# Third places for two page quarters, one wider score product, and a finished result moved by ScalarE

## The chip, the cores and the metric

The kernel runs on one core of one Trainium2 chip. Five engines work side by side: PE (TensorE, matrix products and transposes, with its weight loads shown apart as PEld), DVE (VectorE), ACT (ScalarE), POOL (GpSimd) and SP (SyncE, which here only issues transfers). The metric is the device time in microseconds, the median of several runs.

## What is computed

One inference step of a two-layer decoder: a short-convolution layer, then a layer of native sparse attention, for a prompt of 512 tokens and for 8 samples of 8 new tokens, each sample with 2048 past tokens in a paged cache. All in float32. The part that matters here is the sparse attention of the samples, `nsa_core` of the reference, cut down:

```python
s_c = einsum('bqgrd,bngd->bgrqn', q, kc_blk) * scale            # scores on compressed blocks
p_c = masked_softmax(s_c, blk_end <= q_pos); o_c = p_c @ vc_blk
imp_s = block sums of p_c over the heads of a group
_, idx = top_k(imp_s + forced, 16)                              # 16 blocks of 64 past tokens
s_s = einsum('bqgrd,bgqnkd->bgrqnk', q, kv_g[..., 0, :]) * scale  # selected blocks
o_s = masked_softmax(s_s) @ kv_g[..., 1, :]
s_w = einsum('bqgrd,bkgd->bgrqk', q, kvw[:, :, 0]) * scale      # window of 512 tokens
o_w = masked_softmax(s_w) @ kvw[:, :, 1]
out = gate0 * o_c + gate1 * o_s + gate2 * o_w
```

For a sample the kernel scores all 2048 past tokens and adds a mask for the blocks that were not selected, so it reads all 16 pages of a sample (128 tokens each, 256 KB with keys and values), and its window (512 tokens, 1024 KB).

## The kernel before

The program is one straight stream for each engine, with semaphores set by hand. The stages are: norms and memory keys, the convolution layer, its output product, the projections of the second layer, attention of the prompt (about 700 to 803 us of the profile), attention of the samples (803 to 964 us), the last output product and the final norm.

**The sample stage.** `sample_phase` orders it: front(0), and then for each sample t: middle(t), front(t+1), back(t). `NB` is 8, samples are 0 to 7.

- *front(t)*: PE turns (transposes) the keys of sample t in ten turn tiles, j = 0 to 9, of four transposes each. `TURNED` says of what: tiles 0, 1 are quarter 0, tiles 2, 3 quarter 1, tiles 4, 5 quarter 2, tiles 6, 7 the window, tiles 8, 9 quarter 3. A quarter is four of the 16 pages. ACT and DVE copy the turned keys from PSUM back over the pages (lines 1224 and 2436). Between them PE scores the compressed blocks, and DVE makes the selection mask (lines 2460 to 2469).
- *middle(t)*: PE's scores. First the window part, one 512-column product a head group for the window and two 64-column ones for the new tokens (`new(0)` for the selected branch, `new(1)` for the window branch); then `out_turn`, a transpose of the finished result of sample t-1 into PSUM bank 1; then quarters 2 and 3, then quarters 0 and 1 (32 instructions of 512 columns). The last pair writes banks 0 and 1, so it waits until the result of t-1 was moved out of bank 1.
- *back(t)*: PE turns the 23 tiles of probabilities and multiplies them with the values in six groups of up to four tiles; each group adds one to `sa_used`. Group 1 is compressed blocks and part of the window, groups 2 to 5 are quarters 0 to 3, group 6 the rest. A page's place is free when its group is done.

DVE's stream for one sample: masks and maxima of sample t (`masks`, lines 2479 to 2498, run inside front(t+1)), the copies and the selection mask of front(t+1), then back(t). Its back ended with four small copies (line 2531) that move the turned result from bank 1 into `HT`, the input of the output product.

**The places.** `skv(t, c)` is the memory for quarter c of sample t. Quarter 0 had three places (used by t mod 3), quarters 1, 2 and 3 two (t mod 2); the window has three. The residual stream X (2560 KB) was written to DRAM earlier and came back at 718 us, before the prompt's attention.

**The queues.** SP loads pages 0 and 1 of each quarter and the windows, POOL pages 2 and 3. Both go through their lists in order. `quad_load` (line 583) waits until sample t - 2 (or t - 3) has used the quarter: `sa_used` past that sample's group c + 2. SP's list for t = 1 to 7 was: quarters 1, 2, 3 of t, quarter 0 of t+1, window of t+1. So what SP and POOL issue once a back has come to its last groups is a train: on each queue two pages of quarters 1, 2, 3 and then two of quarter 0, on SP a window behind them. The output weights follow at the end, `load_w(B_OUT1)` and `load_w(B_OUT1 + 1)`, each when its memory is free.

Of the kernel before, what the change touches and what calls it, by code (L numbers as in the profile page):

```python
# [29 lines left out]
SEQ = 512  # L30
NB, NT = 8, 8
# [222 lines left out]
def build(nc, I, O):  # L254
    ctx = ExitStack()
    with ctx:
# [110 lines left out]
        FIRST = [four_pages(a) for a in (at(8192, 2048), at(4096, 2048), shared)]  # L367
        LATER = [[four_pages(at(o, 2048)) for o in quads] for quads in ((10240, 0, 2048), (12288, 14336, 16384))]

        def skv(t, c):  # L370

            return LATER[t % 2][c - 1] if c else FIRST[t % 3]

# [98 lines left out]
        sa_lo = [[sem(f"sa_pages01_{c}_{n}") for n in range(2 if c else 3)] for c in range(4)]  # L472
        sa_hi = [[sem(f"sa_pages23_{c}_{n}") for n in range(2 if c else 3)] for c in range(4)]
# [109 lines left out]
        def quad_load(eng, t, c, pages, loaded):  # L583

            places = 2 if c else 3
            if t >= places:
                eng.wait_ge(sa_used, START.sa_used + 6 * (t - places) + c + 2)
            for s in pages:
                page = eng.value_load(ptab[0:1, NPG * t + 4 * c + s:NPG * t + 4 * c + s + 1], min_val=0, max_val=POOL - 1)  # L589
                eng.dma_start(skv(t, c)[:, s, :], I["csel"][bass.ds(page, 1), :, :].rearrange("a p c -> (a p) c")  # L590
                              ).then_inc(loaded[c][t % places], 16)
# [13 lines left out]
        def _(sp):  # L605
# [138 lines left out]
            sp.dma_start(Xf, x_dram).then_inc(x_back, 16)  # L744
# [38 lines left out]
        def _(pool):  # L783
# [74 lines left out]
            quad_load(pool, 0, 1, range(2, 4), sa_hi)  # L858
            pool.wait_ge(pa_t, BANKS_OF_P * (UNITS - 2))
# [3 lines left out]
            pool.wait_ge(pa_mix, 6)  # L863
            quad_load(pool, 1, 0, range(2, 4), sa_hi)
            for t in range(1, NB):
                for c in range(1, 4):
                    quad_load(pool, t, c, range(2, 4), sa_hi)
                if t + 1 < NB:
                    if t == 1:
# [1112 lines left out]
        def _(dve):  # L1982
# [523 lines left out]
            def back(t, fronts):  # L2506
# [22 lines left out]
                for g in range(KVH):  # L2529
# [3 lines left out]
                    if g < 3:  # L2533
                        lk.did(ins)
# [140 lines left out]
```

## Time and profile before

| | us |
|---|---|
| median of 3 runs | 1040.93 (1040.17 to 1042.69) |
| the profiled execution | 1036.34 |
| its span, first to last instruction | 1034.7 |
| PE busy in the span | 965.7 |
| DVE, ACT, POOL busy | 599.1, 298.2, 70.6 |
| mean granted TensorE clock | 0.982 |
| data moved by DMA | 153.03 MB |

The profile is of one execution. Times in its rows are microseconds from the span's start; each row of a timeline merges instructions of one line that follow each other on an engine, with their number behind an x, and names in brackets the idle time before them and what ended it. L1275 is the line of every product, L1278 of every transpose, L590 of every page load, L737 of the windows. Ends of PE instructions are modelled, so that PE can be shown as busy while it is not at its peak.

### The profile page before, as it was taken

Reading aid. Unit: us, or ns where it says so; the run is one execution under the profiler, and the core shown is the slowest. Engines: PE = TensorE matmul, PEld = TensorE weight load, DVE = VectorE, ACT = ScalarE, POOL = GpSimd, SP = SyncE. Lnnn points to the kernel's source line nnn. Section 1 sums busy time; section 2 is a strip of 40 time slices with the busy share of each in tenths; the row PEclk is TensorE's granted clock in tenths of the full one; section 3 lists DMA queues with packets and bytes.
Section 4 is the critical chain, followed back from the end, with each engine's and each line's share of the span. In section 5 each row is a group of like instructions: output and inputs, shape, how many; then the busy total and the mean of one; then the engine's idle time right before and its main releaser. Section 6 shows DMA issues by size and latency. Waiting matters only on the chain.

```text
span 1034.7 us, 17598 instructions
## 1 busy us (share of the span) xinstructions
PE 965.7 (93%) x6530; PEld 600.6 (58%) x6530; DVE 599.1 (58%) x1356; ACT 298.2 (29%) x734; POOL 70.6 (7%) x133
## 2 busy tenths in 40 slices
PE   5999999999977999999999999989899899998997
PEld 3576676667754445566755555665555666655443
DVE  3204997797543645999914222448876667766113
ACT  4310010100143023112124221347776434435012
POOL 0000000000000000000012010310000222120000
PEclk9999999999988999999999999999999999999999
DMA  8543644554361443386522351453002878774202
GB/s 350 184 101 123 174 122 143 172 161 100 107 206 42 104 141 123 92 212 193 181 82 101 104 185 53 162 218 109 40 1 97 312 239 301 278 247 164 103 2 90
DMA packets 48879, 153.03 MB, mean 148 GB/s; under 512 B 9497, under 2 KB 23194, under 8 KB 41882
## 3 DMA queue, kind: packets, MB, share of 16 engines
q1 hardware_dynamic: 43674, 135.13, 40.8%
q0 software_dynamic: 5120, 16.78, 4.7%
q8 instruction: 52, 0.85, 0.3%
q14 instruction: 33, 0.27, 0.1%
HBM read 142.26 MB, written 17.89 MB: 155 GB/s over the span
## 4 chain that ended last, share of the span: by engine, by line
PE 78%; DVE 8%; DMA 6%; issue 4%; ACT 1%; POOLq 1%; SPq 1%; POOL 0%; DVEq 0%; ACTq 0%
PE PS L1275 70%; PE PS L1278 8%; DMA arena<-in_csel 4%; DVE arena L2190 1%; DVE arena L2396 1%; DMA arena<-in_wall 1%; POOLq L589 1%; DMA arena<-in_cmem 1%; DVE arena L2001 1%; POOL arena L590 0%; DVE arena L2033 0%; DVE arena L2034 0%; ACT arena L1188 0%; DVE arena L2401 0%; SPq L589 0%
## 5 line engine op out<-in xcount | busy, mean ns | idle before, releaser
L1275 PE MATMUL PS<-arena 128*32 128x64 f32 (+16 forms) x5436 | 833.3, 376 | 21.7 <-issue 7.4
L1275 PEld LDWEIGHTS PS<-arena 128*128 128x128 f32 (+6 forms) x5436 | 478.2, 148 | 348.1 <-issue 220.7
L1278 PE MATMUL PS<-arena 128*128 128x128 f32 (+3 forms) x1094 | 150.4, 285 | 39.7 <-ACT arena L898 11.0
L1278 PEld LDWEIGHTS PS<-arena 128*128 128x128 f32 (+3 forms) x1094 | 125.1, 146 | 78.0 <-issue 40.2
L2033 DVE TENSOR_TENSOR arena<-arena 128x2048 f32<-128x2048 f32 x32 | 73.2, 2288 | 3.6 <-DMA arena<-in_ccmp 2.4
L2034 DVE TENSOR_TENSOR arena<-arena 128x2048 f32<-128x2048 f32 x32 | 73.1, 2285 | 0.0
L1051 ACT ACTIVATE arena<-arena 128x512 f32<-128x512 f32 (+3 forms) x96 | 53.0, 555 | 30.1 <-DVE arena L2190 30.0
L2190 DVE CUSTOM_DVE_ANT_0 arena<-PS,arena 128x512 f32<-128x512 f32 (+3 forms) x96 | 41.5, 487 | 20.6 <-PE PS L1275 20.6
L590 POOL DMA_DIRECT2D arena<-in_csel x64 | 34.7, 541 | 209.4 <-PE PS L1278 99.2
L2294 DVE TENSOR_TENSOR arena<-arena,PS 128x512 f32<-128x512 f32 x16 | 11.0, 687 | 57.0 <-PE PS L1275 56.9
L2036 DVE TENSOR_TENSOR arena<-arena 128x1024 f32<-128x1024 f32 x32 | 39.0, 1219 | 0.0
L2038 DVE TENSOR_TENSOR arena<-arena 128x1024 f32<-128x1024 f32 x32 | 39.0, 1219 | 0.0
L1188 ACT COPY arena<-PS 128x512 f32<-128x512 f32 x60 | 32.0, 580 | 11.3 <-PE PS L1278 11.3
L2001 DVE TENSOR_TENSOR arena<-PS,arena 128x512 f32<-128x512 f32 x28 | 17.4, 683 | 23.1 <-PE PS L1278 23.1
L2396 DVE TENSOR_SCALAR arena<-arena 128x128 f32<-128x128 f32 (+1 forms) x96 | 29.5, 382 | 0.4
L1224 ACT COPY arena<-PS 128x512 f32<-128x512 f32 x40 | 22.6, 586 | 19.7 <-PE PS L1278 19.2
L1157 ACT COPY arena<-PS 128x512 f32<-128x512 f32 x16 | 9.4, 587 | 60.1 <-PE PS L1275 60.1
L2335 DVE SCALAR_TENSOR_TENSOR arena<-arena 128x576 f32<-128x576 f32 x8 | 6.2, 797 | 33.5 <-ACT arena L1136 33.5
L1243 ACT ACTIVATE arena<-PS,arena 128x512 f32<-128x512 f32 x8 | 5.5, 688 | 65.0 <-DVE arena L2486 65.0
L1267 ACT ACTIVATE arena<-arena 128x1024 f32<-128x1024 f32 x5 | 5.3, 1057 | 62.4 <-DVE arena L2294 60.1
L811 POOL MEMSET arena<- 64x2048 f32 x1 | 1.8, 1801 | 310.2 <-ACT arena L944 310.2
L1117 ACT ACTIVATE arena<-arena 128x1024 f32<-128x1024 f32 x5 | 5.3, 1058 | 60.5 <-DVE arena L2294 58.6
(207 smaller groups left out, 560.9 us busy)
## 6 DMA issues: line engine op xcount, KB each, us to landing
arena<-in_wall SPq DMA_DIRECT2D x19, 2048.0 KB, 9.6
arena<-in_ccmp SPq DMA_DIRECT2D x128, 256.0 KB, 3.7
arena<-in_csel POOLq DMA_DIRECT2D x64, 256.0 KB, 5.6
arena<-in_csel SPq DMA_DIRECT2D x64, 256.0 KB, 5.1
arena<-in_cmem SPq DMA_DIRECT2D x32, 256.0 KB, 6.1
arena<-in_win SPq DMA_DIRECT2D x8, 1024.0 KB, 9.3
out_win_s<-in_win SPq DMA_DIRECT2D x1, 8064.0 KB
x_scratch<-arena SPq DMA_DIRECT2D x1, 2560.0 KB, 9.3
```

The lines of the kernel that those rows point to most:

```text
L590: eng.dma_start(skv(t, c)[:, s, :], I["csel"][bass.ds(page, 1), :, :].rearrange("a p c -> (a p) c")).then_inc(loaded[c][t % places], 16)
L1051: ins = nc.scalar.activation(S, S, ACT.Exp, bias=unit_stats(u, "max")[:, c:c + 1], scale=-1.0, accum_out=unit_stats(u, "sum")[:, c:c + 1])
L1188: nc.scalar.copy(PT_[u % 2][:, 512 * b:512 * b + 512], PS[:, p_bank("turns", g), :]).then_inc(pa_ca, 1)
L1275: return nc.tensor.matmul(out, lhsT, rhs, start=start, stop=stop, skip_group_check=True)
L1278: return nc.tensor.transpose(out, in_, ident[0:in_.shape[0], 0:in_.shape[0]])
L2001: ins = tt(dst[:, 4 * half:4 * half + 4, :], PS[:, bank, :].rearrange("p (k c) -> p k c", k=4), bc(g[:, 4 * half:4 * half + 4], 128), ALU. ...
L2033: tt(tile_view(made[0]), tile_view(PG[T % 2]), tile_pos("tile_pos0"), ALU.mult).then_inc(cp_a, 1)
L2034: tt(tile_view(made[1]), tile_view(PG[T % 2]), tile_pos("tile_pos1"), ALU.mult).then_inc(cp_b, 1)
L2036: tt(made[0][:, 0:1024], made[0][:, 0:1024], made[0][:, 1024:2048], ALU.add).then_inc(cp_half, 1)
L2038: tt(made[1][:, 0:1024], made[1][:, 0:1024], made[1][:, 1024:2048], ALU.add).then_inc(cp_half, 1)
L2190: ins = causal_add(SP[u % 3][:, 1280 * gg + o:1280 * gg + o + nk], PS[:, score_bank(x, gg) if u else 5 + gg, 0:nk], FUT[:, 512 - nk:512], ...
L2396: ins = ts(S, S, w[:, 4 * gg + ti:4 * gg + ti + 1], None, ALU.mult)
```

## The change

1. *Places.* Quarters 1 and 2 get a third place each, in the first 4096 columns of X's memory (`arena[:, 0:2048]` and `arena[:, 2048:4096]`). Samples use places by t mod 3, but the last sample's quarters 1 and 2 go to the third place (index 2) and not to X's memory, which samples 1 and 4 use. Quarter 3 keeps two places. The semaphores of quarters 1 and 2 become common ones, so the wait for quarter 1 in front is for both.
2. *Order of the loads.* Quarters 1 and 2 of sample 1 are loaded where X was. X comes back when sample 4 is done. For t = 2 to 7 the lists are: quarters 1 and 2 of t, quarter 0 of t+1, window of t (SP alone), quarter 3 of t. The two blocks of output weights change places in time, since their memory gets free in another order.
3. *New tokens.* `new(0)` and `new(1)` become one product of 128 columns.
4. *The finished result.* The four copies of line 2531 go from DVE to ACT, at the end of ACT's back; each now adds one to `sa_done`. DVE's copy of the new tokens' mask (line 2479) moves ahead of its waits.

```diff
+        PAGES = [[four_pages(a) for a in quads] for quads in (
+            (at(8192, 2048), shared, at(4096, 2048)),
+            (at(10240, 2048), arena[:, 0:2048], at(12288, 2048)),
+            (at(0, 2048), arena[:, 2048:4096], at(14336, 2048)),
+            (at(2048, 2048), at(16384, 2048)))]
+        def place(t, c):
+            return 2 if t == NB - 1 and c in (1, 2) else t % len(PAGES[c])
+        def last_in(t, c):
+            return max([s for s in range(t) if place(s, c) == place(t, c)], default=None)
...
-            places = 2 if c else 3
-            if t >= places:
-                eng.wait_ge(sa_used, START.sa_used + 6 * (t - places) + c + 2)
+            last = last_in(t, c)
+            if last is not None:
+                eng.wait_ge(sa_used, START.sa_used + 6 * last + c + 2)
...
             sp.wait_ge(cp_took, NB + 1)
-            sp.dma_start(Xf, x_dram).then_inc(x_back, 16)
+            quad_load(sp, 1, 1, range(2), sa_lo)
+            quad_load(sp, 1, 2, range(2), sa_lo)
...
             sp.wait_ge(pa_mix, 6)
+            sp.wait_ge(state_out, 16)
             quad_load(sp, 1, 0, range(2), sa_lo)
+            quad_load(sp, 1, 3, range(2), sa_lo)
             window(1)
-            for t in range(1, NB):
-                for c in range(1, 4):
-                    quad_load(sp, t, c, range(2), sa_lo)
+            quad_load(sp, 2, 0, range(2), sa_lo)
+            for t in range(2, NB):
+                if t == NB - 1:
+                    sp.wait_ge(sa_used, START.sa_used + 6 * (NB - 3))
+                    sp.dma_start(Xf, x_dram).then_inc(x_back, 16)
+                quad_load(sp, t, 1, range(2), sa_lo)
+                quad_load(sp, t, 2, range(2), sa_lo)
                 if t + 1 < NB:
-                    if t == 1:
-                        sp.wait_ge(state_out, 16)
                     quad_load(sp, t + 1, 0, range(2), sa_lo)
-                    window(t + 1)
+                window(t)
+                quad_load(sp, t, 3, range(2), sa_lo)
+            sp.wait_ge(sa_used, START.sa_used + 6 * (NB - 2))
+            load_w(B_OUT1 + 1)
             sp.wait_ge(sa_used, START.sa_used + 6 * (NB - 1))
             load_w(B_OUT1)
-            sp.wait_ge(sa_used, START.sa_used + 6 * (NB - 1) + 2)
-            load_w(B_OUT1 + 1)
...
+                act.wait_ge(sa_y, t.value(1, 1, base=START.sa_y))
+                for g in range(KVH):
+                    o, gp = 64 * (g % 2), g // 2
+                    nc.scalar.copy(HT[o:o + 64, 2 + gp:7 + gp:2, bass.ds(t.at(NT, SEQ), NT)],
+                                   PS[0:HD, 1, 32 * g:32 * g + 24].rearrange("p (r t) -> p r t", r=GRP)
+                                   ).then_inc(sa_done, 1)
...
-                def new(s):
-                    return 5, 128 + 64 * s, 64, lambda p, gp: Kn[p:p + 64, s, gp, :]
-                both([(4, 0, 512, lambda p, gp: SWKT[p:p + 64, gp, :])], [new(0), new(1)]).then_inc(sa_part, 1)
+                new = [(5, 128, 128, lambda p, gp: Kn[p:p + 64, :, gp, :])]
+                both([(4, 0, 512, lambda p, gp: SWKT[p:p + 64, gp, :])], new).then_inc(sa_part, 1)
```

POOL's list changes as SP's does, without the windows, X and weights.

## Rows read from the trace of the kernel before

**Rows 1.** Page, chain that ended last: share of the span by engine.
```profile
PE 78%; DVE 8%; DMA 6%; issue 4%; ACT 1%; POOLq 1%; SPq 1%; POOL 0%; DVEq 0%; ACTq 0%
```

**Rows 2.** Windows, one sample: PE, PEld, DVE, ACT, POOL busy; clock; DMA; GB/s.
```profile
869.00:888.00 19.00, 16.94 (x291) 11.49 (x286) 13.52 (x58) 8.39 (x17) 4.28 (x9) 1.00 0.79 278
```

**Rows 3.** Waits of PE, 803 to 965 us: total, times, longest.
```profile
PE PS L1278 <- DMA arena<-in_csel: 7.3, 10, 1.6
```

**Rows 4.** Timeline of PE: start, us, instructions, idle before.
```profile
822.98 2.40 PE L1278 MATMUL PS<-arena 128*128 128x128 f32 x20 [1.28 <-DMA arena<-in_csel]
...
843.13 0.63 PE L1278 MATMUL PS<-arena 128*128 128x128 f32 x4 [0.39 <-DVE arena L2436]
...
871.79 3.65 PE L1275 MATMUL PS<-arena 64*32 64x512 f32 x32
875.37 1.09 PE L1278 MATMUL PS<-arena 128*128 128x128 f32 x8
...
878.36 1.94 PE L1278 MATMUL PS<-arena 128*128 128x128 f32 x16 [0.57 <-DMA arena<-in_csel]
881.02 0.63 PE L1278 MATMUL PS<-arena 128*128 128x128 f32 x4 [0.72 <-DMA arena<-in_csel]
...
884.75 2.37 PE L1275 MATMUL PS<-arena 127*32 127x64 f32 x135
...
938.26 0.63 PE L1278 MATMUL PS<-arena 128*128 128x128 f32 x4 [0.74 <-DMA arena<-in_csel]
```

**Rows 5.** Timeline of SP's issues: start, us until the last was issued.
```profile
804.83 1.43 SPq L590 DMA_DIRECT2D arena<-in_csel  x2
806.30 0.44 SPq L737 DMA_DIRECT2D arena<-in_win  x1
...
831.07 8.20 SPq L590 DMA_DIRECT2D arena<-in_csel  x8
...
868.30 8.00 SPq L590 DMA_DIRECT2D arena<-in_csel  x8
...
925.96 6.15 SPq L590 DMA_DIRECT2D arena<-in_csel  x6
```

**Rows 6.** Timeline of POOL's issues: the sixth of a train.
```profile
874.82 0.54 POOL L590 DMA_DIRECT2D arena<-in_csel  x1 [0.61 <-issue]
```

**Rows 7.** Single issues at 806.30, 809.00, 838.94, 874.82, 875.97: KB, us to landing.
```profile
arena<-in_win SPq DMA_DIRECT2D x1, 1024.0 KB, 9.3
arena<-in_csel SPq DMA_DIRECT2D x1, 256.0 KB, 10.3
arena<-in_csel SPq DMA_DIRECT2D x1, 256.0 KB, 6.5
arena<-in_csel POOLq DMA_DIRECT2D x1, 256.0 KB, 6.1
arena<-in_csel SPq DMA_DIRECT2D x1, 256.0 KB, 6.9
```

**Rows 8.** Windows in a train, columns as in rows 2.
```profile
868.00:875.00 7.00, 6.63 (x113) 2.27 (x102) 3.47 (x19) 0.76 (x3) 2.87 (x6) 1.00 0.77 254
875.00:881.00 6.00, 4.72 (x42) 3.92 (x37) 5.63 (x17) 4.40 (x10) 1.44 (x3) 1.00 1.02 369
```

**Rows 9.** Windows over the window part of sample 7, columns as in rows 2.
```profile
945.20:945.65 0.45, 0.45 (x19) 0.27 (x12) 0.27 (x1) 0.00 (x0) 0.00 (x0) 1.00 0.00 0
945.65:946.10 0.45, 0.45 (x6) 0.11 (x1) 0.30 (x2) 0.00 (x0) 0.00 (x0) 1.00 0.00 0
```

**Rows 10.** Timeline of DVE: the four copies, a score step, the last four copies.
```profile
871.90 0.79 DVE L2531 COPY arena<-PS 64x24 f32<-64x24 f32 x4 [2.17 <-PE PS L1278]
...
875.52 0.69 DVE L2494 CUSTOM_DVE_ANT_1 arena<-PS,arena 128x512 f32<-128x512 f32 x1
...
963.00 0.79 DVE L2531 COPY arena<-PS 64x24 f32<-64x24 f32 x4 [0.39 <-PE PS L1278]
```

**Rows 11.** A line of ACT, copies from PSUM: min/median/max ns.
```profile
L944 ACT COPY arena<-PS x8: 377/377/378, 150.6 to 537.1; 127x256 f32<-127x256 f32 x8
```

More of the change, by code:

```diff
@@ L365, in four_pages, with times @@
             return a.rearrange("p (s c) -> p s c", s=4)
-        FIRST = [four_pages(a) for a in (at(8192, 2048), at(4096, 2048), shared)]
-        LATER = [[four_pages(at(o, 2048)) for o in quads] for quads in ((10240, 0, 2048), (12288, 14336, 16384))]
+        PAGES = [[four_pages(a) for a in quads] for quads in (
[7 more added lines that the diff above has]
+            return max([s for s in range(t) if place(s, c) == place(t, c)], default=None)
+        def times(t, c):
+            return sum(place(s, c) == place(t, c) for s in range(t + 1))
         def skv(t, c):
-            return LATER[t % 2][c - 1] if c else FIRST[t % 3]
+            return PAGES[c][place(t, c)]
         SWKT = at(18432, 1024).rearrange("p (g c) -> p g c", g=2)
@@ L471, in build @@
         fut_set = sem("future_set")
-        sa_lo = [[sem(f"sa_pages01_{c}_{n}") for n in range(2 if c else 3)] for c in range(4)]
-        sa_hi = [[sem(f"sa_pages23_{c}_{n}") for n in range(2 if c else 3)] for c in range(4)]
+        sa_lo, sa_hi = [[[sem(f"sa_pages{h}_{c}_{n}") for n in range(len(PAGES[c]))] for c in (0, 1, 3)] for h in ("01", "23")]
+        sa_lo.insert(2, sa_lo[1])
+        sa_hi.insert(2, sa_hi[1])
         (sa_cs, sa_cm, sa_ce, sa_cn, sa_imp, sa_mask, sa_ft, sa_fa, sa_fd, sa_s, sa_m, sa_p,
@@ L590, in quad_load @@
                 eng.dma_start(skv(t, c)[:, s, :], I["csel"][bass.ds(page, 1), :, :].rearrange("a p c -> (a p) c")
-                              ).then_inc(loaded[c][t % places], 16)
+                              ).then_inc(loaded[c][place(t, c)], 16)
         def sample_phase(front, middle, back):
@@ L858, in _ @@
             quad_load(pool, 0, 1, range(2, 4), sa_hi)
+            pool.wait_ge(cp_took, NB + 1)
+            quad_load(pool, 1, 1, range(2, 4), sa_hi)
+            quad_load(pool, 1, 2, range(2, 4), sa_hi)
             pool.wait_ge(pa_t, BANKS_OF_P * (UNITS - 2))
@@ L863, in _ @@
             pool.wait_ge(pa_mix, 6)
+            pool.wait_ge(state_out, 16)
+            pool.wait_ge(gates_written, 16)
             quad_load(pool, 1, 0, range(2, 4), sa_hi)
[L865 to L867 removed]
+            quad_load(pool, 1, 3, range(2, 4), sa_hi)
+            quad_load(pool, 2, 0, range(2, 4), sa_hi)
+            for t in range(2, NB):
+                quad_load(pool, t, 1, range(2, 4), sa_hi)
+                quad_load(pool, t, 2, range(2, 4), sa_hi)
                 if t + 1 < NB:
[L869 to L871 removed]
                     quad_load(pool, t + 1, 0, range(2, 4), sa_hi)
+                quad_load(pool, t, 3, range(2, 4), sa_hi)
         @block.scalar
@@ L1868, in front @@
                         if k % 2 == 0:
-                            places = 2 if k else 3
-                            pe.wait_ge(sa_lo[k // 2][number % places], 32 * (number // places + 1))
-                            pe.wait_ge(sa_hi[k // 2][number % places], 32 * (number // places + 1))
+                            c, loads = k // 2, 64 if k // 2 in (1, 2) else 32
+                            pe.wait_ge(sa_lo[c][place(number, c)], loads * times(number, c))
+                            pe.wait_ge(sa_hi[c][place(number, c)], loads * times(number, c))
                         for q in range(2):
@@ L2527, in back @@
                 stt(SO, PS[:, 0, 0:HD], rs(158, 159), SO, ALU.mult, ALU.add).then_inc(sa_mix, 1)
-                dve.wait_ge(sa_y, t.value(1, 1, base=START.sa_y))
-                for g in range(KVH):
-                    o, gp = 64 * (g % 2), g // 2
-                    ins = tcopy(HT[o:o + 64, 2 + gp:7 + gp:2, bass.ds(t.at(NT, SEQ), NT)],
-                                PS[0:HD, 1, 32 * g:32 * g + 24].rearrange("p (r t) -> p r t", r=GRP))
-                    if g < 3:
-                        lk.did(ins)
-                ins.then_inc(sa_done, 1)
             dve.wait_ge(kv_stored, KV_STORED)
```

10 lines of the change are left out of this document (4 added, 6 removed).

## The prediction

> **What bounds the kernel now.** I read the page first: the chain that ended last is 78% PE and 6% DMA [rows 1], so time is set by PE and by what PE waits for. Everything that the diff moves belongs to the sample stage (803 to 965 us), so the views after that are of this stage. In the window of one sample PE is busy 16.94 us of 19.00 and the DMA engines 79% [rows 2]: two resources near their limits. In the waits PE loses 7.3 us to page loads, in 10 waits [rows 3]. The timeline shows where: 1.28 us in front 1, 0.57 and 0.72 in front 4, and so on to 0.74 at the last one, in front 7; front 2 waits 0.39, put down to a DVE copy [rows 4].
>
> Why does it wait? Take the back of sample 2, which ends near 868.9. Its value groups free the places of quarters 1 to 3, and SP starts its train at 868.30 [rows 5]: two pages each of quarters 1, 2, 3 of sample 4, of quarter 0 of sample 5, then a window; POOL issues the other two pages of each. POOL's last page of quarter 3 is issued at 874.82 and lands 6.1 us later, at 880.9 [rows 6, 7]. PE starts turn tile 8, the first of quarter 3, at 881.02 [rows 4]: 12.72 us after the train's first issue. For the first and the last such front, 2 and 7, the same distance is 843.13 - 831.07 = 12.06 and 938.26 - 925.96 = 12.30 [rows 4, 5]; the six lie between 12.06 and 12.72, and fronts 2 to 5 average 12.45. Without the two waits PE would have come to tile 8 at 11.4. This is the loop to watch: values end, train, quarter 3 lands, ten more PE steps, values end. A period lasts as long as the train's last urgent page plus a fixed rest.
>
> **The train after the change.** Quarters 1 and 2 get a third place, so for samples 2 to 6 they are no longer urgent: they land a period early. What stays tied to the back just ending is quarter 3 (two places) and, new, the window: it was loaded a period ahead and is now loaded for the front at hand. SP's train becomes: two pages of quarter 0 (next sample), window (a megabyte, four pages' worth), two pages of quarter 3, then two pages each of quarters 1 and 2 of the next sample. POOL's is two pages each of 0, 3, 1, 2. Up to quarter 3 SP's queue holds eight page lengths, where it held six.
>
> When does the eighth length land? SP's eighth page, issued at 875.97, took 6.9 us [rows 7], so it landed 14.6 us after 868.30, with POOL's eight pages beside it; in the first of the five such trains it landed 14.4 after (issued 838.94, 6.5 us, from 831.07) [rows 5, 7], and 14.8 is their mean. There is also a train of exactly the new shape: at 804.83 SP issued two pages, a window, then pages [rows 5]. The window took 9.3 us, and the second page behind it (issued 809.00) 10.3 [rows 7]: landed at 819.3, 14.5 after the first issue. What stands behind the window lands behind it. Against these, the window puts a megabyte on SP's queue at once, where pages come 1.1 us apart; but the DMA engines were already 77% busy in 868 to 875, with the first data only after about 1.3 us, and 102% in 875 to 881 [rows 8], so little can be won: I take 14.2. From below, the pages needed up to quarter 3 are still twelve lengths over both queues; were SP's served first, they would end as twelve do now, near 12.4.
>
> The Trainium skill, "DMA: Bandwidth & Descriptors", section "Queues, rings and completion order", says that each DMA engine takes turns between the rings that have work and takes descriptors of one ring in order. By this, SP's eight lengths would end together with POOL's eight pages, at 14.6 to 14.8, which is the dear rival below; the train at 804.83 agrees with the order within a ring.
>
> The train also begins earlier: quarter 0 waits for two value groups, quarter 1 waited for three. The values of a back run 135 instructions in 2.37 us [rows 4], a group of 32 in 0.55. So quarter 3 lands at 14.2 - 0.55 = 13.65 where PE now starts at 12.45: **+1.2 in each of fronts 2 to 5, +4.8** (bounds: 12.4 gives -0.6, 14.8 gives +1.8).
>
> Front 1: two of its quarters now come at about 717 instead of the X reload, long before. Its other pages and window are the first eight lengths of the train at 804.83, done by 819.3, before PE asks: **-1.3** (the 1.28 of rows 4; 0 at worst).
>
> Front 6: POOL's quarters 1 and 2 of sample 7 now wait for the back of sample 5, since this sample's place is the third one. So POOL has four pages only, SP eight lengths: twelve in all, as today up to quarter 3. 12.3 less 0.55 against 12.28: **-0.6** (at most the 1.09 that it waits). The X reload (2.6 MB) follows on SP's queue; at 369 GB/s [rows 8] it takes 7.1 us and ends near 19.5 us after the train's start, when the next train's data begin: nothing, at most +1.
>
> Front 7: SP's train is quarters 1 and 2, window, quarter 3: ten lengths, POOL's six pages, all needed: sixteen, today's whole train. 14.4 against 12.30: **+2.1** (0.9 to 2.7). That quarters 1 and 2 share semaphores makes tile 2 wait for both; tile 8 is later still.
>
> **The other edits.** The 128-column product: eight 512-column and sixteen 64-column instructions of the window part end in four steps of 0.45; the second step has only six instructions beginning or running on [rows 9], the tail of the 512-column ones, so the 64-column ones run under them. Eight of 128 columns do too: 0, at most -0.1 a sample, and behind a DMA wait nothing.
>
> ScalarE's copies: DVE's four took 0.79, after which its mask work began; its step on the scores of quarter 0, at 875.52, followed PE's scores, which end as tile 0 starts at 875.37 [rows 4, 10]. DVE can begin about 1 us sooner (the copies' 0.79 and the turn that they wait for) and still stops there for PE: 0. ScalarE's price is not in the trace; the nearest are DVE's 0.79 for four and its own PSUM copy of 256 columns, 0.377 [rows 11], 1.5 for four. Begun at 871.90 that ends by 873.4; PE needs bank 1 only in the second half of the 32 products that begin at 871.79 and last 3.65 [rows 4], from 873.6. Behind these copies on ScalarE stands the window's exponential, which waits for DVE's masks anyway: 0. Only at the end nothing covers them: DVE's last four began at 963.00 [rows 10] and the gating product follows. **+0.4** (0 to +0.7). The output weights load sooner, but PE's products do not wait for them now: 0.
>
> **Sum.** -1.3 + 4.8 - 0.6 + 2.1 + 0.4 = +5.4 us. The profiled execution took 1036.34 (span 1034.7 and 1.6 around it): 1041.7. The median of the runs, 1040.93, lies 4.6 above that execution; I add the difference to the median: **1046.3 us**. A measurement of this kernel tells a change from none at about 0.3%, 3.1 us.
>
> **Rivals.** *Covered loads (faster).* If quarter 3 lands before 11.4 us after today's train start, the waits of fronts 1 to 6 go: the 7.3 in all, and front 2's 0.4, less 0.9 that front 7 keeps, make -6.8; with +1.0 in front 7 and +0.4 at the end -5.4: 1035.5. For it: three fifths of the bytes are no longer urgent. Against: SP's queue of eight lengths, and the train at 804.83. It decides at 12.45; sooner than this each front gains. Chance 0.22.
> *Even.* Quarter 3 lands about where it does now: -1.3 + 0 - 0.6 + 1.3 + 0.4, about -0.2: 1040.7. For it: the same twelve lengths are needed first, from a start 0.55 earlier. Against: POOL's next four pages compete. Chance 0.26.
> *Dear train (slower than forecast).* No relief at all, 14.8: +1.8 in four fronts, -0.4 in front 6, +2.7 and +0.7: -1.3 + 7.2 - 0.4 + 2.7 + 0.7 = +8.9: 1049.8. For it: the five trains' eighth pages, and equal turns of the two queues. Chance 0.12.
> *Forecast.* 0.40. All of it and the dear train are slower by more than 0.3%, covered loads faster, the even case within: faster 0.22, same 0.26, slower 0.52. The range, 1035.5 to 1050.5, reaches from covered loads to the dear train, whose far halves it leaves out; within the forecast's own case (14.0 to 14.5) the time is 1044.5 to 1048.5.
>
> **What would show it.** Right: in each of fronts 2 to 5 PE waits some 2.2 us (13.65 - 11.4) at tile 8 for pages that SP issued behind a window and that land about 14 us after the train's first issue; none in front 1; a wait of 3 us or so in front 7; periods near 20 us; DVE's masks begin before PE's turn of the finished result and stop at the scores; the window part as long as before. Wrong: page waits under 5 us in all, or a landing of quarter 3 by 12 us, which would mean that SP's queue gets more than half of the DMA engines while POOL's has work; or a new wait on ScalarE's copies at the third pair of score products.

## The result, and the profile after

The change makes the kernel slower, by more than the prediction's range held:

| kernel | us, median (range) | before beside it | ratio, 95% interval |
|---|---|---|---|
| changed | 1061.44 (1054.92 to 1064.70), 4 runs | 1041.81 | 1.0178 (1.0125 to 1.0232) |
| changed, measured again (7 below) | 1058.41 (1055.74 to 1060.28), 4 runs | 1043.56 | 1.0138 (1.0092 to 1.0185) |

So +15 to +20 us, where +5.4 was forecast. The first profiled execution took 1054.92 (span 1053.2, mean granted clock 0.969). All times of the changed kernel's rows are later by 4.7 when the sample stage begins. That is not the change: front 0's first transposes started at 802.1 to 808.9 in the fourteen profiles of this study, whatever the kernel. From there to the first output product the stage lasts 172.41 us (808.87 to 981.28) against 160.24 before (804.20 to 964.44).

After's page, the chain that ended last by engine; in [rows 1] DMA held 6%:
```profile
PE 78%; DVE 8%; DMA 7%; issue 4%; ACT 2%; SPq 1%; POOLq 0%; POOL 0%; DVEq 0%; ACTq 0%
```
After's waits of PE, 803 to 985 us, beside [rows 3] (total, times, longest). Fewer and longer: three waits for pages, two for windows, of up to 4.0 us, and three more that stand against a copy or nothing, because the transfer had landed 0.1 us before they ended:
```profile
PE PS L1311 <- DMA arena<-in_csel: 9.4, 3, 4.0
PE PS L1311 <- DMA arena<-in_win: 5.4, 2, 3.7
...
PE PS L1311 <- issue: 3.5, 3, 2.4
...
PE PS L1311 <- DVE arena L2471: 1.7, 1, 1.7
PE PS L1311 <- ACT arena L1251: 1.7, 1, 1.7
```
After's timeline of PE, fronts 3, 4 and 7, beside [rows 4]. The groups of 8 are tiles 6 and 7, those of 4 tile 8, the 27 what follows (tile 9 and the back's turns); the 28 of front 7 are tiles 2 to 8:
```profile
864.23 1.06 PE L1311 MATMUL PS<-arena 128*128 128x128 f32 x8 [1.72 <-ACT arena L1251]
867.72 1.08 PE L1311 MATMUL PS<-arena 128*128 128x128 f32 x4 [2.43 <-issue]
...
869.02 4.95 PE L1311 MATMUL PS<-arena 128*128 128x128 f32 x27
...
889.16 1.30 PE L1311 MATMUL PS<-arena 128*128 128x128 f32 x8 [3.69 <-DMA arena<-in_win]
892.18 1.09 PE L1311 MATMUL PS<-arena 128*128 128x128 f32 x4 [1.72 <-DVE arena L2471]
...
893.49 4.67 PE L1311 MATMUL PS<-arena 128*128 128x128 f32 x27
...
951.56 4.78 PE L1311 MATMUL PS<-arena 128*128 128x128 f32 x28 [4.00 <-DMA arena<-in_csel]
...
956.40 3.11 PE L1311 MATMUL PS<-arena 128*128 128x128 f32 x27
```
The same 27 transposes take 3.11 us in one front and 4.95 or 4.67 in another. After's windows tell why (columns as in [rows 2]; third from the right is the granted clock, then the DMA share):
```profile
868.00:875.00 7.00, 7.00 (x91) 6.61 (x93) 3.54 (x22) 3.52 (x6) 0.00 (x0) 0.66 0.18 64
885.00:893.00 8.00, 2.58 (x17) 2.01 (x16) 3.00 (x6) 2.05 (x3) 0.12 (x1) 0.80 0.93 349
893.00:899.00 6.00, 6.00 (x75) 5.61 (x77) 3.45 (x21) 3.52 (x6) 0.00 (x0) 0.69 0.02 8
```
Behind a long wait PE is granted 0.66 or 0.69 of its clock, a mixture of its two levels, 1.2 and 2.4 GHz: it works without a pause and gets less done. And the DMA engines, 93% busy while PE waits, are 2% busy right after. This suggests that the bytes fit into the period and come in the wrong order; experiments 1 and 12 test it.

The train behind front 4's waits, after's SP issues and POOL's last, beside [rows 5, 6]:
```profile
876.06 1.53 SPq L606 DMA_DIRECT2D arena<-in_csel  x2
877.63 0.43 SPq L753 DMA_DIRECT2D arena<-in_win  x1
878.82 6.22 SPq L606 DMA_DIRECT2D arena<-in_csel  x6
```
```profile
884.59 0.54 POOL L606 DMA_DIRECT2D arena<-in_csel  x1 [0.61 <-issue]
```
After's landings of single issues, beside [rows 7]: the window of 877.63, quarter 3's second page of 879.92, the page of 881.02 behind it, POOL's last of 884.59:
```profile
arena<-in_win SPq DMA_DIRECT2D x1, 1024.0 KB, 11.4
arena<-in_csel SPq DMA_DIRECT2D x1, 256.0 KB, 12.2
arena<-in_csel SPq DMA_DIRECT2D x1, 256.0 KB, 10.0
arena<-in_csel POOLq DMA_DIRECT2D x1, 256.0 KB, 7.3
```
The window lands 13.0 us after the train's first issue, quarter 3 16.1 after it; POOL's eighth page, which nobody needs yet, 15.8 after. PE had come to tile 6 at 885.47, 9.4 after.

### The profile page after: what moved, and what is told of

Same layout as the page of the kernel before. It is cut to its first block, busy times and chain, and to the rows that moved or that the text cites. A ratio compares the mean times of both kernels' runs of the same rounds, so it can differ in the third digit from the quotient of the medians.

```text
span 1053.2 us, 17463 instructions
## 1 busy us (share of the span) xinstructions
PE 972.1 (92%) x6466; PEld 607.4 (58%) x6466; DVE 594.0 (56%) x1324; ACT 304.2 (29%) x766; POOL 70.4 (7%) x133
## 4 chain that ended last, share of the span: by engine, by line
PE 78%; DVE 8%; DMA 7%; issue 4%; ACT 2%; SPq 1%; POOLq 0%; POOL 0%; DVEq 0%; ACTq 0%
PE PS L1308 69%; PE PS L1311 9%; DMA arena<-in_csel 3%; DMA arena<-in_win 2%; DVE arena L2222 2%; DVE arena L2428 1%; DMA arena<-in_wall 1%; DMA arena<-in_cmem 1%; DVE arena L2033 1%; SPq L605 1%; SPq L606 0%; DVE arena L2065 0%; DVE arena L2066 0%; DVE arena L2526 0%; ACT arena L1215 0%
## 5 line engine op out<-in xcount | busy, mean ns | idle before, releaser
L1308 PE MATMUL PS<-arena 128*32 128x64 f32 (+13 forms) x5372 | 831.9, 380 | 19.5 <-issue 5.3
L1308 PEld LDWEIGHTS PS<-arena 128*128 128x128 f32 (+4 forms) x5372 | 477.1, 149 | 348.6 <-issue 222.3
L1311 PE MATMUL PS<-arena 128*128 128x128 f32 (+3 forms) x1094 | 158.2, 295 | 54.1 <-ACT arena L925 10.8
L1311 PEld LDWEIGHTS PS<-arena 128*128 128x128 f32 (+3 forms) x1094 | 133.0, 152 | 89.2 <-issue 53.0
L1215 ACT COPY arena<-PS 128x512 f32<-128x512 f32 x60 | 32.0, 579 | 11.0 <-PE PS L1311 10.9
L2033 DVE TENSOR_TENSOR arena<-PS,arena 128x512 f32<-128x512 f32 x28 | 17.4, 683 | 23.9 <-PE PS L1311 23.9
L2526 DVE CUSTOM_DVE_ANT_1 arena<-PS,arena 128x512 f32<-128x512 f32 x32 | 20.8, 686 | 9.9 <-issue 9.9
```

The costliest lines, as they stand in the source:

```text
L1215: nc.scalar.copy(PT_[u % 2][:, 512 * b:512 * b + 512], PS[:, p_bank("turns", g), :]).then_inc(pa_ca, 1)
L1308: return nc.tensor.matmul(out, lhsT, rhs, start=start, stop=stop, skip_group_check=True)
L1311: return nc.tensor.transpose(out, in_, ident[0:in_.shape[0], 0:in_.shape[0]])
L2033: ins = tt(dst[:, 4 * half:4 * half + 4, :], PS[:, bank, :].rearrange("p (k c) -> p k c", k=4), bc(g[:, 4 * half:4 * half + 4], 128), ALU. ...
```

## Theories

*Theory A.* With the window loaded for the front at hand, eight page lengths on SP's queue are urgent, and they share the DMA engines with POOL's eight pages, of which four are not. The waits grow to as much as 4 us, and behind some of them PE runs at half clock, a cost of its own. *Rivals:* the bytes of a train set the time in any order; quarter 3's place behind the window is what counts, not the window; the low clock is by the way; the small edits cost something.

The stage (start of front 0's first transposes to first output product) in the profile of each kernel, for reference below. The kernels ran on several chips; the ratio is to the kernel before, run beside each, and so is the better measure between experiments of different numbers:

| kernel | stage, us | time, median us | ratio to before, interval |
|---|---|---|---|
| before, first and second profile (the second is 11) | 160.24, 164.28 | 1041 to 1044 | |
| changed, first and second profile (the second is 7) | 172.41, 179.43 | 1061.44, 1058.41 | 1.0178, 1.0138 |
| 1 window a period ahead | 154.37 | 1032.77 | 0.9917 (0.9863 to 0.9970) |
| 2, 10 PE busy in the waits, twice | 174.64, 178.18 | 1046.64, 1053.39 | 1.0058 (0.9997 to 1.0118), 1.0096 (1.0070 to 1.0122) |
| 3 POOL holds back | 161.73 | 1040.33 | 0.9990 (0.9932 to 1.0047) |
| 4 small edits alone | 164.28 | 1044.66 | 1.0023 (0.9963 to 1.0083) |
| 5 places and loads alone | 154.62 | 1036.59 | 0.9939 (0.9907 to 0.9970) |
| 6 weights later | 154.89 | 1032.97 | 0.9899 (0.9863 to 0.9934) |
| 8 the same work behind the waits | 183.39 | 1061.97 | 1.0173 (1.0127 to 1.0219) |
| 9 busy in two other waits | 148.23 | 1028.57 | 0.9874 (0.9851 to 0.9897) |
| 12 quarter 3 ahead of the window | 182.66 | 1061.80 | 1.0181 (1.0150 to 1.0212) |

## The experiments

The numbers are those of the order in which the kernels ran; 10 stands with 2, and 11 with 7.

**1. The window a period ahead again.** The changed kernel, SP's list alone reordered (the load of X, left out here, now follows the last window):
```diff
+            quad_load(sp, 2, 1, range(2), sa_lo)
+            quad_load(sp, 2, 2, range(2), sa_lo)
+            window(2)
             for t in range(2, NB):
...
-                quad_load(sp, t, 1, range(2), sa_lo)
-                quad_load(sp, t, 2, range(2), sa_lo)
                 if t + 1 < NB:
                     quad_load(sp, t + 1, 0, range(2), sa_lo)
-                window(t)
+                else:
+                    quad_load(sp, t, 1, range(2), sa_lo)
+                    quad_load(sp, t, 2, range(2), sa_lo)
                 quad_load(sp, t, 3, range(2), sa_lo)
+                if t + 2 < NB:
+                    quad_load(sp, t + 1, 1, range(2), sa_lo)
+                    quad_load(sp, t + 1, 2, range(2), sa_lo)
+                if t + 1 < NB:
+                    window(t + 1)
...
```


> The changed kernel with SP's train reordered: quarter 0 of the next sample, quarter 3, quarters 1 and 2 of the next sample, and only then the next sample's window, a period ahead as in the kernel before (the last train stays as it was, with the window already there). Theory A (the window standing ahead of quarter 3 on SP's queue makes both late): quarter 3 is the fourth length on SP's queue instead of the eighth and lands about 8 us after the train's first issue, PE waits for pages only in front 7 (about 1 us), and the sample stage is some 5 us shorter than that of the kernel before: 1035 to 1038 us. Rival B (what counts is the bytes of a whole train over both queues, in whatever order): waits of 2 us and more stay in fronts 2 to 5, 1050 to 1060 us.

1032.77 us: faster than the kernel before, and 2.2 us below A's lower number. Its waits of PE, 803 to 985 us, and the landings of quarter 3's second page (issued 870.14, train from 866.44) and of the window (issued 875.08):
```profile
PE PS L1319 <- DMA arena<-in_csel: 2.0, 1, 2.0
PE PS L1319 <- DVE arena L2479: 1.7, 1, 1.7
```
```profile
arena<-in_csel SPq DMA_DIRECT2D x1, 256.0 KB, 5.3
...
arena<-in_win SPq DMA_DIRECT2D x1, 1024.0 KB, 9.1
```
SP's second page of quarter 3 lands 9.0 us after the train's first issue. Only front 7 waits, 3.7 in all. The bytes are the same, so the first rival falls: the places are a gain once the window is not urgent.

**2 and 10. PE busy in the waits.** The changed kernel with throwaway transposes ahead of page and window waits:
```diff
+KEEP = {(2, 6): 16, (3, 8): 12, (3, 6): 14, (4, 8): 24, (4, 6): 10, (5, 6): 16, (6, 8): 10, (7, 2): 24}
...
+                    for n_more in range(KEEP.get((number, k), 0)):
+                        turn(PS[:, FRONT_BANK[j], 128 * (n_more % 4):128 * (n_more % 4) + 128], ident)
```
(The second number is what is turned: 8 the window, tile 6; 6 quarter 3's first half, tile 8; 2 quarter 1.)

> The changed kernel with 126 throwaway transposes of a constant (10 to 24 at a place, about 0.115 us each) that PE does just ahead of its page and window waits in fronts 2 to 7, so that it stands idle for less than about 1.5 us in each. Theory A (PE's granted clock falls to half after it has stood idle for nearly 4 us, and this is a good part of what the change costs): waits plus throwaway work last as long as the waits did, the 27 transposes after them take 3.1 us and not 4.7 to 4.9, the granted clock of the sample stage is 0.97 or more, and the kernel takes 1053 to 1057 us. Rival B (the low clock has another reason, or is only by the way): the transposes after the waits stay at 4.7 us or more, 1061 to 1065 us.

1046.64 us, less than A said. Front 3 in its timeline, waits still there, the 27 at full speed (the group of 22 ends with 14 throwaway ones):
```profile
859.95 2.62 PE L1312 MATMUL PS<-arena 128*128 128x128 f32 x22 [2.26 <-DMA arena<-in_win]
863.64 0.66 PE L1312 MATMUL PS<-arena 128*128 128x128 f32 x4 [1.07 <-DMA arena<-in_csel]
...
864.36 3.11 PE L1312 MATMUL PS<-arena 128*128 128x128 f32 x27
```
The interval was wide, so it was run again as 10. (The ratio of the changed kernel that its expectation names is that of experiment 7, 1.0138.)

> The kernel of the second experiment once more, in more rounds, since its interval left open whether it is slower than the kernel before. If the waits alone (without half clock) are what is left of the change, it should come near the 5.4 us of the sum in the prediction, with some throwaway work that no wait covers on top: ratio 1.004 to 1.010. If it comes at or above 1.013, the ratio of the changed kernel in the third call, the earlier result was of that chip.

1053.39 us, ratio 1.0096: slower than before for certain, and 0.4 to 0.8% under the two measurements of the changed kernel. Where a wait of 4.17 us was left over in front 3 of this run's profile, the 26 behind it took 4.54 us. Both medians are below the changed kernel's, by 0.4 to 1.2% of the kernel before, and the mean granted clock of the runs is up (0.972 to 0.987 against 0.961 to 0.969). The profiles don't place that gain in the sample stage: 174.64 and 178.18 us are no shorter than the changed kernel's 172.41 and 179.43, since part of the 14.5 us of throwaway work (126 times 0.115) comes on top, and the profiled execution of 2 was ahead already when the stage began (802.07 against 808.87). What is shown is that the work behind the waits keeps full clock; how much time that saves is not.

**3. POOL holds back.** In POOL's loop, ahead of quarters 1 and 2:
```diff
+                if t > 2:
+                    pool.wait_ge(sa_lo[3][place(t - 1, 3)], 32 * times(t - 1, 3))
                 quad_load(pool, t, 1, range(2, 4), sa_hi)
```


> The changed kernel, but POOL issues its pages of quarters 1 and 2 of the next sample only once SP's two pages of quarter 3 of this sample have landed. Theory A (the two queues share the DMA engines, so POOL's pages that nobody needs yet take time from the window and quarter 3): the window and quarter 3 land about 2 us sooner, fronts 2 to 5 wait 2 us less each, 1047 to 1054 us. Rival B (SP's queue sets its own pace, whatever POOL does): landings of 14 to 16 us after the train's first issue as they were, 1060 to 1063 us; slower still if the held pages come late for the front after.

1040.33 us, 18 to 21 below the changed kernel and more than A said. Waits, and the landing of quarter 3's second page (issued 868.02, train from 863.89):
```profile
PE PS L1313 <- DMA arena<-in_win: 5.2, 4, 1.9
...
PE PS L1313 <- DMA arena<-in_csel: 2.8, 1, 2.8
```
```profile
arena<-in_csel SPq DMA_DIRECT2D x1, 256.0 KB, 8.4
```
It lands 12.5 us after the first issue, near the 12.4 that the prediction took as its lower bound for "SP's served first"; in the changed kernel it lands 13.8 to 16.7 after in fronts 2 to 5 of both profiles, 15.1 on the mean against 12.6 here. So POOL's four early pages take 2.5 us from what is urgent. No wait is now over 2 us but front 7's, and most of the half clock goes with them.

**4. The small edits alone.** The kernel before with parts 3 and 4 of the change.

> The kernel before with the two small edits alone: the new tokens' scores in one 128-column product, and ScalarE's four copies of the finished result in place of DVE's (with DVE's mask copy moved ahead of its waits). No new places, the old order of loads. Theory A (they are worth nothing, +0.4 at the end): 1041 to 1043 us, within 0.3% of the kernel before. Rival B (the copies delay the third pair of score products, or what stands behind them on ScalarE): 0.5 us or more in each of seven samples, 1045 us or more.

1044.66 us, within what can be told from no change; the stage is as long (164.28) as in the second profile of the kernel before. That does not mean that the wider product is worth nothing to PE. The values and the window part behind front 7, where PE waits for nothing, up to the turn of the finished result, in the first profile before and in the first after:
```profile
941.99 5.21 PE L1275 MATMUL PS<-arena 127*32 127x64 f32 x208
947.13 0.30 PE L1278 MATMUL PS<-arena 128*64 128x128 f32 x1
```
```profile
959.44 4.54 PE L1308 MATMUL PS<-arena 127*32 127x64 f32 x200
963.90 0.30 PE L1311 MATMUL PS<-arena 128*64 128x128 f32 x1
```
5.14 us became 4.46. The window part alone, from its first 512-column product to that turn, takes 1.88 us or more in every sample of the three profiles with two 64-column products (before, 11 and 5), and 1.21 in 55 of 77 samples of the eleven with one (the others 1.6 to 2.8). In this experiment the waits took it back: PE's waits put down to page loads are 12.2 us, against 7.7 in the second profile of the kernel before.

**5. Places and loads alone.** Experiment 1 without parts 3 and 4.

> The reordered kernel of the first experiment without the two small edits: the new tokens' scores again in two 64-column products, and DVE again copies the finished result. What is left of the change is the third places and the order of loads. Theory A (the small edits are worth nothing while something covers them, and 0.4 us at the end): within 0.3% of the reordered kernel, 1031 to 1035 us, with the window part of PE as long. Rival B (without page waits there is no cover, and the copies on DVE or the products now show): 0.5 us or more in each sample, 1037 us or more; or, if ScalarE's copies cost more than DVE's, 1029 us or less.

1036.59 us. The median lies 3.6 to 3.8 above those of experiments 6 and 1; the intervals of the ratios overlap. The window part is not as long as there, which A had said: 1.88 us against 1.21 (experiment 4), so PE's rows bear B out for the wider product. The stages are equal within 0.3 us (154.62 against 154.37), but by chance: here the last back's 19 transposes ran at full clock (2.29 us against 4.32) and front 7 did not wait, while a wait of 2.44 behind front 6 was followed by half clock. How much of the 3.8 is the product is not shown. ScalarE's copies cost nothing that shows. After's end, where nothing covers ACT's copies (rows of ACT and DVE; [rows 10] has DVE's 0.79):
```profile
979.88 0.76 ACT L1292 COPY arena<-PS 64x24 f32<-64x24 f32 x4 [4.12 <-PE PS L1311]
980.67 0.56 DVE L2568 TENSOR_TENSOR arena<-arena 128x384 f32<-128x384 f32 x1 [1.18 <-ACT arena L1292]
```
From the last turn of the result to the output product it is 1.74 us (979.54 to 981.28); before it was 1.78.

**6. The weights later.** Experiment 1, and ahead of `load_w(B_OUT1 + 1)` SP waits for quarter 3 of the last sample (both of its semaphores).

> The reordered kernel of the first experiment, but SP issues the first megabytes of the output weights only when quarter 3 of the last sample has landed (they stood right behind its pages on SP's queue). Theory A (the weights, issued 0.6 us before POOL's last page, took part of the DMA engines from it): that page lands in about 6.5 us instead of 8.6, PE's waits in front 7 fall from 3.7 to about 1.5 us, 1030 to 1032 us. Rival B (the weights only fill what is free): the page takes 8 us or more as before, no difference; or the weights now come too late for the output product, which would show as a wait of PE behind the last sample.

Landing of POOL's last page, in experiment 1 and then here:
```profile
arena<-in_csel POOLq DMA_DIRECT2D x1, 256.0 KB, 8.6
```
```profile
arena<-in_csel POOLq DMA_DIRECT2D x1, 256.0 KB, 5.6
```
The weights did take 3 us from it, as A says, and front 7 waits 1.80 instead of 3.7. The time, 1032.97, just above A's 1032, does not show it: front 6 waits 1.16 in this profile.

**7 and 11. Both kernels again.** The changed kernel:

> The changed kernel itself once more, on the chip of the experiments beside it, for a comparison on one chip and a second profile of it. Expected if the first measurement stands: 1057 to 1065 us, granted clock 0.960 to 0.970 over the span, half clock behind waits of 3.5 us and more in two or three of fronts 2 to 7. If instead it comes out within 5 us of the kernel before, the first measurement was of that chip, and the reasons found so far fall.

It repeated (1058.41, clock 0.966 to 0.967 in all four runs), with half clock in more places than expected: in fronts 2 to 5, where two waits stand close together (3.4 to 4.7 us in all), and in front 7 behind 3.65. Front 5 of its profile, the longest window wait:
```profile
915.01 1.94 PE L1311 MATMUL PS<-arena 128*128 128x128 f32 x8 [3.76 <-DMA arena<-in_win]
...
918.82 4.54 PE L1311 MATMUL PS<-arena 128*128 128x128 f32 x27
```
And the kernel before:

> The kernel before itself, for a second profile of it: the first was of an execution of 1036.3 us, while its runs beside the experiments had a median of 1041 to 1044. Expected: page waits of 8 to 12 us in all instead of 7.3 (the kernel with the small edits alone showed 12.2), and a sample stage 3 to 6 us longer. If the sample stage is as long as in the first profile, the difference lies ahead of it.

The stage is 4.0 us longer than in its first profile, but the page waits are hardly more; 2.91 of them is one wait, in front 1 (1.28 in [rows 4]):
```profile
PE PS L1278 <- DMA arena<-in_csel: 7.7, 8, 2.9
```
So of the differences below, which go against the first profile, 4 us are that execution's own luck: 2.0 in front 1 and 1.8 in fronts 2 to 5, by the turns of the finished result.

**8. The same work behind the waits.** The same loop, moved behind the waits for the page or window.

> The changed kernel with the same 126 throwaway transposes as in the second experiment at the same places, but behind PE's page and window waits instead of ahead of them, so that PE stands idle as long as in the changed kernel and then has 14.5 us more to do. Theory A (keeping PE at work during the waits is what brought the time down to 1046.6): 1073 to 1082 us, with half clock behind the waits. Rival B (added transposes change the timing of the loads in some other way that happens to help): 1060 us or less.

1061.97 us: neither number. Fronts 2, 5 and 7 are 2.6 to 2.9 us longer than in the changed kernel's second profile, front 3 2.2, as added work on the path would be; but the 46 transposes behind the window's wait lie under the next wait, which I had counted as added, and front 4 had no wait at all (62 transposes in one run) and was 4.6 shorter:
```profile
889.77 7.13 PE L1312 MATMUL PS<-arena 128*128 128x128 f32 x62
...
896.95 3.11 PE L1312 MATMUL PS<-arena 128*128 128x128 f32 x27
```
Why front 4's train met PE in time here was not followed up. Against experiments 2 and 10, which have the same instructions ahead of the waits, it is 9 to 15 us slower and its stage (183.39) 5 to 9 us longer: the waits hide work, and this alone says little of the clock.

**9. Busy in two waits that no load causes.** Experiment 6, with throwaway transposes into bank 7 where PE waits anyway, the 18 in the first middle ahead of its wait for the masks, the 26 in the last back between `turns(0)` and `turns(1)`:
```diff
+                if number == 0:
+                    for m in range(18):
+                        turn(PS[:, 7, 128 * (m % 4):128 * (m % 4) + 128], ident)
...
+                    for m in range(26):
+                        turn(PS[:, BACK_BANK[1], 128 * (m % 4):128 * (m % 4) + 128], ident)
```


> The kernel of the experiment with the later weights, and PE does throwaway transposes of a constant in two waits that no load causes: 18 in the first sample before its scores (PE waits 2.98 us there for DVE's masks, in every profile so far) and 26 in the last back before the turns of the probabilities (3.2 us for ScalarE's exponential). What PE waits for is the same in both kernels. Theory A (half clock follows an idle wait of 3 us, whatever ended it): the first 48 score products take 5.5 us instead of 6.42, the 19 transposes of the last back 2.3 instead of 3.9, and the kernel is 2 to 2.6 us shorter, 1030 to 1031 us. Rival B (half clock has to do with the loads, or comes by the time of the run): both groups as long as before, the same time or up to 1 us more.

Windows over the first 48 score products and the 19 transposes, in experiment 6 and then here:
```profile
814.91:821.33 6.42, 6.42 (x49) 2.49 (x50) 2.61 (x13) 1.10 (x4) 2.15 (x4) 0.73 1.03 387
951.96:955.88 3.92, 3.92 (x23) 3.75 (x27) 1.40 (x6) 1.88 (x4) 0.00 (x0) 0.57 0.02 4
```
```profile
811.97:816.70 4.73, 4.73 (x50) 1.65 (x50) 2.65 (x14) 1.11 (x4) 2.15 (x4) 1.00 0.97 342
944.13:946.42 2.29, 2.29 (x23) 2.12 (x27) 1.37 (x6) 1.78 (x4) 0.00 (x0) 1.00 0.00 0
```
The same work, 3.3 us less (6.42 + 3.92 - 4.73 - 2.29), with the clock at 1.00 in place of 0.73 and 0.57, and one of the two has no load anywhere near it. 1028.57 us, the fastest version here, 1.3% under the kernel before; its median is 4.4 under that of experiment 6, which ran on another chip, and the intervals of the two ratios overlap, so the gain in time is not shown clear of noise. The 48 products took 6.42 us in all ten other profiles with the wider product, and only here 4.73: there the low clock follows the idle wait. (Of these 1.7 us 1.0 reaches the turn at the end of front 1; a later wait for DVE's masks takes the rest.) The 19 transposes are weaker evidence, since they took 2.29 us in three profiles without throwaway work too (experiments 5, 8 and 12).

**12. Quarter 3 ahead of a window that stays urgent.** One swap of two lines in SP's loop: `quad_load(sp, t, 3, ...)` before `window(t)`.

> The changed kernel with one swap on SP's queue: quarter 3 ahead of the window, which is still loaded for the front at hand. Theory A (that the window became urgent is what costs: eight page lengths on SP's queue are needed for the front at hand, in whichever order): quarter 3 lands about 9 us after the train's first issue, but the window only after 13 to 14.5 us, PE waits 3 to 4.5 us at turn tile 6 and not at tile 8, with half clock behind it, 1056 to 1064 us. Rival B (quarter 3's place behind the window is what costs, and the window has time enough): waits under 1.5 us a front, 1035 to 1043 us.

Waits, the part of the timeline for front 3, and the landings of quarter 3's second page (issued 880.90) and the window (881.27) of the train that began at 877.12:
```profile
PE PS L1311 <- DMA arena<-in_win: 27.3, 6, 6.3
```
```profile
868.57 2.79 PE L1311 MATMUL PS<-arena 128*128 128x128 f32 x12 [6.34 <-DMA arena<-in_win]
...
871.59 3.46 PE L1311 MATMUL PS<-arena 128*128 128x128 f32 x27
```
```profile
arena<-in_csel SPq DMA_DIRECT2D x1, 256.0 KB, 5.6
...
arena<-in_win SPq DMA_DIRECT2D x1, 1024.0 KB, 11.1
```
SP's pages of quarter 3 are there after 9.4 us, the window after 15.3, and the time is that of the changed kernel. What costs is that the window became urgent, not which of the two stands first. The waits at tile 6 are longer than A said (4.6 to 6.3 in fronts 2 to 5).

## Why the prediction was right in direction and wrong in size

Step by step, in us. Measured are the stretches from the stage's start over the turns of the finished result (836.61 at the end of front 1 and so on to 963.90 at that of front 7, in the first profile after) to the first output product, against those of the first profile before:

| term | forecast | first profile after | second |
|---|---|---|---|
| front 1 | -1.3 | -2.8 | -2.4 |
| fronts 2 to 5 | +4.8 | +10.9 | +17.4 |
| front 6 | -0.6 | +0.3 | +0.4 |
| front 7 | +2.1 | +3.7 | +3.6 |
| the end | +0.4 | +0.1 | +0.1 |
| sum | +5.4 | +12.2 | +19.2 |

- *Direction and place: right in the main.* Quarter 3 comes late behind the window, there is no wait in front 1, the largest loss is in fronts 2 to 5 and then front 7, and ScalarE's copies cost nothing. Not foreseen was that PE stops for the window itself, at tile 6: 5.4 of the 15.0 us of waits in fronts 2 to 5, and 8.6 of 16.6 in the second profile. Experiments 1 and 12 show the cause by taking it away and by leaving it in another order.
- *The step that failed: "I take 14.2", the landing of quarter 3, in "+1.2 in each of fronts 2 to 5, +4.8".* It landed 15.1 us after the train's first issue on the mean, later than the dear train's 14.8. PE's waits in these four fronts add up to 15.0 and 16.6 in the two profiles, against 4.2 before (four times 12.45 - 11.4): +10.8 and +12.4 where +4.8 was put. The choice leant on trains whose eighth page on SP's queue nobody waited for, and on "so little can be won" from a full queue; POOL's share was weighed in the rivals alone, for the dear one and against the even one. Experiment 3 shows that it belonged in the forecast: without POOL's early pages quarter 3 lands after 12.6 on the mean. Put into the prediction's own sum (less 0.55, against 12.45, four times), the mean landings of the two profiles, 14.76 and 15.43, make +7.0 and +9.7 in place of +4.8. The prediction set the rule of the Trainium skill, "DMA: Bandwidth & Descriptors", section "Queues, rings and completion order", against the forecast; in the eight trains SP's eight lengths and POOL's eight pages ended 15.1 and 15.8 us after the first issue on the mean, never more than 1.8 apart, near to what it would have.
- *A term that was missing: PE's clock.* The forecast priced a wait at its own length. Behind the waits of fronts 3, 4 and 7 in the first profile, and of 2 to 5 and 7 in the second, the transposes ran slower: beyond their 3.11, 0.63 and 1.06 us the groups of 27, 4 and 8 in fronts 2 to 5 took 4.5 us more in the first profile and 9.2 in the second, and front 7's 28 another 1.6 (4.78 against 3.23). With the +7.0 and +9.7 that makes 11.5 and 18.9, where 10.9 and 17.4 were measured. Experiment 9 shows the low clock behind a wait that no load causes, and that work in it takes the low clock away. The Trainium skill, "TensorE: Matmul & The Clock Gate", section "HAM oscillation — how this bites in real kernels", says that PE falls back to half clock in a wait for data and begins the next burst cold; these rows agree, but for two waits of the first profile, 2.62 us in front 2 and 2.80 in front 5, behind which the 27 took 3.11 as at full clock. The kernel before stayed clear of it in the sample loop, where its first profile has no page wait over 1.6 us [rows 3].
- *A term put at nothing with a wrong reading: the 128-column product.* The prediction read the 64-column instructions as running under the 512-column ones, "0, at most -0.1 a sample", and took "the window part as long as before" as a sign of being right. It became 0.67 us shorter (1.88 to 1.21, experiment 4). In the changed kernel this bought nothing in fronts 2 to 5: PE came to the loads sooner and waited longer. From the first value product to the turn of the finished result these fronts took 23.9 us in all before and 19.2 and 19.1 after, of which the product is 2.7; the rest of that 4.7 was not traced. So the waits grew by more (10.8 and 12.4) than the later landings alone account for (7.0 and 9.7).
- *Front 1* gained more than its wait: the first sample's score products, at half clock behind a wait of 2.98, took 6.42 us with the wider product against 6.94. Of the rest, 0.6 to 1.0, most of it lies between the first value product and the turn of the result (6.29 us before, 5.48 and 5.95 after).
- *Front 6*: quarter 3 landed 12.3 after the first issue as said, but the window, 11 after, made PE wait 1.75 at tile 6; *front 7*: 1.6 of its 3.7 is half clock. It waits at tile 2 until 951.56 for quarter 2, though quarter 1's last page was there at 946.5; separate semaphores for the two were not tried. The output weights, put at 0, take 3 us from POOL's last page in the order of experiment 1 (experiment 6).
- *The rivals.* "Covered loads" needed quarter 3 by 11.4 us: experiment 1 has all four pages at 9.5 to 9.6 in fronts 2 to 5, and ends at 1032.77, below that rival's 1035.5; without the small edits it is 1036.59 (experiment 5). The change held that gain, and the window's place gave it away. The inner range "1044.5 to 1048.5" for landings of 14.0 to 14.5 does not follow from the sum, which gives 1045.5 to 1047.5; nothing hangs on it.

## What to carry to other kernels

When a buffer is added so that some loads need not be in time, list again what is now urgent on each queue, and keep off every queue, until it has landed, what is not: here the same bytes in another order make 1.8% slower or 0.8% faster. Price a long wait of the matrix engine with the work behind it at half clock as well, and read the granted clock of the stretch after each such wait before summing. Where a wait can't be removed, throwaway transposes in it kept the clock up here; whether they pay is shown for the first scores of experiment 9 (1.7 us there, 1.0 at the end of front 1), and not for the waits of experiments 2 and 10. And an edit that total time calls worthless may only be covered: look at the length of its own rows.

## What the runs showed that I had not expected

- Transposes alone, throwaway ones in a wait of 2.98 us, left the granted clock at 1.00 for the products behind them, where it had been 0.73 (experiment 9).
- The same wait of 3.2 us in the last back was followed by 3.1 to 4.3 us for the 19 transposes in ten profiles, and by the 2.29 of full clock in three (experiments 5, 8 and 12). One profile does not tell whether a wait costs clock.
- Of two pages on SP's queue the earlier can land later: 879.92 + 12.2 is 892.1, the one behind it, 881.02 + 10.0, is 891.0. That was so by 0.6 us or more in 3 of the 8 trains of fronts 2 to 5 in the two profiles after, and quarter 3 landed over a range of 2.9 us.
